# Kept key products, a scaled state on ScalarE, and reordered attention projections in a two-layer hybrid backbone

## The chip, the cores and the metric

The program runs on one core of one Trainium2 chip. Its metric is the device time of one execution in microseconds (us). A core has TensorE (PE, with its weight loads shown as PEld), VectorE (DVE), ScalarE (ACT), GpSimd (POOL) and the DMA queues, most of them issued by SyncE (SP). The engines run side by side, each through its own list of instructions in order, and meet only at semaphores.

## The reference

One inference step of a two-layer backbone, for 512 latent tokens and 128 context tokens together (640 columns). Each layer runs three head groups on one normalised input: a bidirectional chunked gated DeltaNet, latent attention (MLA), and windowed attention with a sink. Their outputs go through one projection, and a squared-ReLU MLP follows. The change is in the preparation of the two attentions and in the DeltaNet recurrence:

```python
kb = kc * bc[..., None]
lower = jnp.where(strict, jnp.einsum('nbhik,nbhjk->nbhij', kb, kc) * decay, 0.0)
...
intra = jnp.where(incl, jnp.einsum('nbhik,nbhjk->nbhij', qc, kc) * decay, 0.0)
def step(S, inp):
    v_new = u_i - jnp.einsum('bhck,bhkv->bhcv', w_i, S)
    o_i = (jnp.einsum('bhck,bhkv->bhcv', q_i * jnp.exp(g_i)[..., None], S)
           + jnp.einsum('bhij,bhjv->bhiv', a_i, v_new))
    S = (S * jnp.exp(g_last)[..., None]
         + jnp.einsum('bhck,bhcv->bhkv', k_i * jnp.exp(g_last - g_i)[..., None], v_new))
...
q_m = (_rms_norm(m_cq, g) @ w_uq)         # per head 64 plain columns and 32 that are rotated
q_rope = _apply_rope(q_rope, cos_m, sin_m)
k_nope, v_m = _mla_expand(ckv_n, w_ukv)
```

The recurrence runs forward over the latent blocks and, with its own decays, backward. The products `k k^T` and `q k^T` of a block are the same for both directions.

## The kernel before, in words

All activations are feature-major: 128 features on the partitions, tokens in the columns. The kernel works in blocks of 128 tokens: four latent blocks 0 to 3 and the context block 4 (`LB` is 4, `NB` is 5). Every engine has its list written out by hand, and `wait_ge` and `then_inc` on named semaphores tie the lists together; a wait holds back all that stands behind it on its engine. No scheduler moves anything.

**Attention preparation** (lines 2588 to 2655 on TensorE, 1233 to 1265 on ScalarE, 1976 to 1991 on VectorE). TensorE turns the values and keys of the DeltaNet into token-major form (`QKV`, `KTOK`), multiplies latent keys and queries by a permutation (`rr`) so that VectorE can rotate them with `rotate(n, ...)` (`rot`), and then projects: `queries` three times (two groups of plain columns, then the rotated columns `QR`), `keys` twice, the values `VM` and the turned window values `SVT`. ScalarE copies each result out of PSUM (`pev`). The rotated queries `QR` go from ScalarE to a permutation on TensorE, to VectorE (`rotate(4, ...)`), and to GpSimd, which copies them into `QT` (`qrc`). Then the score matmuls `scores_a` (L2660) begin.

**Attention rounds** follow: eight rounds of scores, softmax, turned weights and values, then the context block.

**Recurrence.** `blocks[s]` gives the block of step s for direction d: forward 0, 1, 2, 3 and backward 3, 2, 1, 0, and both take block 4 at the end. In one step (loop `for s in range(LB - 1)`) the state part of step s and the preparation of step i = s + 1 are interleaved:

- TensorE: `key_state` (L2860, state times grown keys `KE`), `key_products(i, 0)` (L2748), `solve` (L2873), `key_products(i, 1)`, `query_state` (L2882), `first_product(i, 0)` (L2763), `update` (L2898), `corner_product`, `second_product`, `own_values` (L2890).
- VectorE: `right_side` (`XS`), `scaled_decays` (`DTB`, L2092), `decayed(i, 0)` (`CM` and `AT` from the key products in PSUM, L2107), `solution` (`VN`, L2168), `decayed(i, 1)`, `masked` (`DT`, L2084), `state` (`SS`, L2188: four instructions, each old state times its decay plus the update), `output` (`OACC`), and small copies between.
- GpSimd: `KE` and `QE` (L858), `VS` (L890), and the spreads `UU` and `TT` (L842, L850).
- ScalarE: the decays (`gate_less`, `gate_grown`, `gate_decay`) and half of the small copies.

`first_product(i, 0)` waits for `CM` and `AT` of both directions (`cm`, `atm`). The next `key_state` waits for the state (`sst`) and for the output copied out of the bank that it writes (`oa`).

Step i = 1 needs the products of blocks 1 and 2, step 2 those of 2 and 1, step 3 those of 3 and 0: in steps 2 and 3 TensorE makes again what steps 0 and 1 had. The weight buffer `RAW` holds two chunks of 1 MB and `X` the residual input; `refill(g)` loads chunk g + 2 into `RAW[g % 2]`.

## Time and profile before

| | |
|---|---|
| median of 3 runs | 1798.57 us (1796.0 to 1802.94) |
| the profiled execution | 1795.4 us, of it the span of the profile 1793.6 us |
| busy share of the span | PE 96%, PEld 92%, DVE 70%, ACT 47%, POOL 29% |
| mean granted TensorE clock | 0.99 |

The page gives the span in engines, in 40 slices, in a chain of waits and in groups of instructions. Layer 0 prepares its attentions at 261 to 283 us, runs the rounds to 350 and the recurrence to 425; layer 1 does the same at 1139 to 1161, 1228 and 1303. A timeline row gives start and length of a group of like instructions, and in brackets the idle time of the engine ahead of it with what ended it. The end of a row of matmuls lies a little over the start of the next row, since matmuls are pipelined.

### The profile page before, as it was taken

How to read it: one execution, taken by the hardware profiler on the slowest of the kernel's cores; microseconds unless marked ns; L12 is line 12 of the kernel's file. 1: busy time of each engine (PE TensorE's matmuls, PEld its weight loads, DVE VectorE, ACT ScalarE, POOL GpSimd, SP SyncE). 2: the span in 40 equal slices, each digit the busy share in tenths (PEclk: the TensorE clock that was granted, in tenths of full speed). 3: DMA queues.
4: the chain of work that ended last, by engine and by line, in shares of the span. 5: the costliest groups of instructions: out<-in, count | busy, mean ns of one | idle time of the engine just before them, and what ended most of it. 6: DMA issues, size and time to landing. Idle time of an engine off the chain costs nothing.

```text
span 1793.6 us, 33484 instructions
## 1 busy us (share of the span) xinstructions
PE 1730.5 (96%) x13554; PEld 1649.8 (92%) x13554; DVE 1263.6 (70%) x2087; ACT 846.4 (47%) x1455; POOL 521.8 (29%) x418
## 2 busy tenths in 40 slices
PE   5999999999999999999999999999999999999997
PEld 2889996789999999999999999778899999999997
DVE  2688776798635776776665557668987777788885
ACT  1555427744342231322325653476446665756663
POOL 5000002174441140421551000215822323333235
PEclk9999999999999999999999999999999999999998
DMA  8653213023557779687527861651133677887662
GB/s 341 255 211 104 79 60 83 2 67 120 202 190 244 290 222 336 234 269 290 182 71 213 187 147 48 141 95 55 38 112 118 218 252 234 306 291 244 225 205 83
DMA packets 128037, 316.66 MB, mean 177 GB/s; under 512 B 37828, under 2 KB 64236, under 8 KB 108172
## 3 DMA queue, kind: packets, MB, share of 16 engines
q1 hardware_dynamic: 121740, 279.49, 44.6%
q0 software_dynamic: 4608, 33.56, 9.6%
q8 instruction: 108, 1.77, 0.4%
q10 hardware_dynamic: 1536, 1.48, 0.2%
q14 instruction: 45, 0.37, 0.1%
HBM read 286.01 MB, written 95.49 MB: 213 GB/s over the span
## 4 chain that ended last, share of the span: by engine, by line
PE 82%; DVE 8%; DMA 3%; issue 3%; ACT 3%; SPq 1%; POOL 0%; POOLq 0%; DVEq 0%; ACTq 0%
PE PS L2389 48%; PE PS L2458 19%; DMA ADA<-ada 1%; PE PS L2660 1%; PE PS L2748 1%; PE PS L2706 1%; PE PS L2685 1%; PE PS L2890 1%; PE PS L2674 1%; DVE MPR L1812 1%; PE PS L2526 1%; PE PS L2694 1%; PE PS L2898 1%; PE PS L2873 1%; PE PS L2860 1%
## 5 line engine op out<-in xcount | busy, mean ns | idle before, releaser
L2389 PE MATMUL PS<-HH,HI 128*128 128x320 f32 (+1 forms) x1280 | 299.9, 316 | 5.2 <-DVE HL L1561 5.2
L2389 PE MATMUL PS<-HL,HI 128*128 128x320 f32 (+1 forms) x1280 | 295.4, 312 | 0.0
L2389 PE MATMUL PS<-HH,LO 128*128 128x320 f32 (+1 forms) x1280 | 293.5, 310 | 0.0
L957 ACT CAST HI<-RAW 128x2048 fp32r<-128x2048 f32 x64 | 121.9, 1904 | 274.0 <-PE PS L2389 246.8
L2389 PEld LDWEIGHTS PS<-HH,HI 128*128 128x128 f32 x1280 | 215.3, 190 | 5.8 <-issue 5.7
L2389 PEld LDWEIGHTS PS<-HL,HI 128*128 128x128 f32 x1280 | 219.3, 191 | 0.0
L2389 PEld LDWEIGHTS PS<-HH,LO 128*128 128x128 f32 x1280 | 217.1, 190 | 0.0
L2458 PE MATMUL PS<-FB,WHL 128*128 128x320 f32 x1344 | 199.4, 309 | 5.3 <-DVE TMP L1689 2.4
L2458 PE MATMUL PS<-HB,WHL 128*128 128x322 f32 (+1 forms) x1344 | 202.5, 313 | 2.1 <-DVE TMP L1689 1.5
L2458 PEld LDWEIGHTS PS<-FB,WHL 128*128 128x128 f32 x1344 | 197.1, 188 | 7.6 <-DVE WHL L1606 5.4
L2458 PEld LDWEIGHTS PS<-HB,WHL 128*128 128x128 f32 x1344 | 201.7, 191 | 2.4 <-issue 2.4
L1004 ACT CAST WHL<-RAWB 128x512 fp32r<-128x512 f32 x224 | 137.7, 618 | 111.3 <-PE PS L2458 92.7
L1552 DVE TENSOR_TENSOR LO<-RAW,HI 128x2048 fp32r<-128x2048 f32 x62 | 149.0, 2404 | 56.1 <-ACT HI L957 55.8
L2389 PE MATMUL PS<-FH,HI 128*128 128x320 f32 x768 | 175.8, 310 | 1.6 <-issue 1.6
L1606 DVE TENSOR_TENSOR WHL<-RAWB,WHL 128x512 fp32r<-128x512 f32 x224 | 168.6, 778 | 8.9 <-ACT WHL L1004 7.3
L2389 PE MATMUL PS<-FH,LO 128*128 128x320 f32 x768 | 174.6, 309 | 0.0
L2389 PE MATMUL PS<-FL,HI 128*128 128x320 f32 x640 | 145.7, 309 | 0.0
L1812 DVE SCALAR_TENSOR_TENSOR MPR<-WM,CB 128x1024 f32<-128x1024 f32 x96 | 137.9, 1437 | 9.5 <-DMA WM<-adt 7.8
L2389 PEld LDWEIGHTS PS<-FH,HI 128*128 128x128 f32 x768 | 127.9, 188 | 2.0 <-issue 1.1
L2389 PEld LDWEIGHTS PS<-FH,LO 128*128 128x128 f32 x768 | 128.3, 188 | 0.0
L2389 PEld LDWEIGHTS PS<-FL,HI 128*128 128x128 f32 x640 | 107.1, 188 | 0.0
L933 POOL TENSOR_TENSOR TC<-TC 128x640 f32<-128x640 f32 x32 | 50.4, 1576 | 181.3 <-ACT FH L1497 181.3
(380 smaller groups left out, 2874.9 us busy)
## 6 DMA issues: line engine op xcount, KB each, us to landing
RAW<-ws SPq DMA_DIRECT2D x64, 1024.0 KB, 5.1
wp<-ws SPq DMA_DIRECT2D x32, 1024.0 KB, 8.2
RAWB<-wp SPq DMA_DIRECT2D x128, 256.0 KB, 4.0
WM<-adt SPq DMA_DIRECT2D x48, 512.0 KB, 9.2
RAWB<-ws SPq DMA_DIRECT2D x96, 256.0 KB, 3.9
FS<-hb SPq DMA_DIRECT2D x28, 640.0 KB, 8.6
ADA<-ada SPq DMA_DIRECT2D x16, 1024.0 KB, 7.8
wp<-ws POOLq DMA_DIRECT2D x16, 1024.0 KB, 10.1
```

The source lines that it names most:

```text
L933: nc.gpsimd.tensor_tensor(TC[u][:, 0:T], TC[u][:, 0:T], TC[u][:, 0:T], ALU.mult).then_inc(S["f1_sq"], 1)
L957: nc.scalar.copy(HI[g % 2][:, :], RAW[g % 2][:, :]).then_inc(hi_ready, 1)
L1004: nc.scalar.copy(WHL[:, w % SLOTS, 0, :], operand(w)).then_inc(F["whi"], 1)
L1552: last = nc.vector.tensor_tensor(LO[g % 2][:, c], RAW[g % 2][:, c], HI[g % 2][:, c].bitcast(F32), ALU.subtract)
L1606: nc.vector.tensor_tensor(WHL[:, w % SLOTS, 1, :], operand(w), WHL[:, w % SLOTS, 0, :].bitcast(F32), ALU.subtract).then_inc(F["wlo"], 1)
L1812: return nc.vector.scalar_tensor_tensor(out=MPR[:, :], in0=w[:, :], scalar=1.0, in1=cond[:, g, :], op0=ALU.mult, op1=ALU.mult, accum_out=M ...
L2389: last = pe.matmul(bank(2 * u + a)[:, 0:e], w[:, cols], m[:, a * HT:a * HT + e], start=(k == 0 and f), stop=(k == KT - 1 and e_))
L2458: last = pe.matmul(out, x[:, cols], B[:, y, k, 0:n], start=(opens and k == 0 and v == 0), stop=(k == H - 1 and v == 2), skip_group_check=n ...
L2526: last = pe.matmul(bank(7)[:, 464 + i * NB + b:465 + i * NB + b], SQT[i % 2][:, c.start - 1:c.stop - 1], one, start=True, stop=True)
L2660: pe.matmul(pair(0)[:, 0:LAT], q, kt[:, 0:LAT], start=True, stop=True)
L2674: last = pe.matmul(bank(7 if i else 2)[:, c:c + hi - lo], TSQ[rows, p, toks(b)], KSW[rows, lo:hi], start=True, stop=True)
L2685: last = pe.transpose(pair(2)[:, toks(i)], TC[a % 2][:, toks(slot)], ident)
```

## The change

Five edits, in both layers:

1. ScalarE copies the key products of steps 0 and 1 out of PSUM into four SBUF tiles `KK` (`products_out`, by block), and TensorE makes none for steps 2 and 3. `decayed(2, ...)` and `decayed(3, ...)` read `KK`. `decayed` of step 1 and of (0, 0) waits for ScalarE's copies; TensorE waits for them too at four places (`kte` + 5, 6, 8).
2. ScalarE multiplies the state by its decay beforehand (`state_decay`, four instructions into `SD`), and `state` on VectorE is one addition.
3. The rotated queries are projected first; their copy, permutation and rotation come before the other queries and keys; waits stand later or are split, and one new one is there (`rot` + 5 before the second `keys`).
4. The last copy of turned values on ScalarE goes ahead of the last projection tile's bias activations.
5. `KK` and `SD` lie in `RAW[0]` and in `X`, so the load of chunk 12 and the load of half of `X` are issued later.

```diff
+        KK = [place(f"KK{b}", [P, H, 2, P], F32, w) for b, w in enumerate((r_raw, r_x, r_x + 4096, r_raw + 4096))]
+        SD = [place(f"SD{d}", [P, H, P], F32, (r_x + 8192, r_kd)[d]) for d in range(2)]
 ... SyncE
-                        if s % 2 == 0 and s // 2 + 1 < PT_ // 2 - 1:
+                        if s % 2 == 0 and s // 2 + 1 < PT_ // 2 - 2:
                             refill(g0 + s // 2 + 1)
...
-                    sp.dma_start(X[:, 0:4, :, :], ...)
                     for i in range(2, NB):
                         ...
                         gates_in(i)
+                    sp.wait_ge(S["cm"], o["cm"] + 8)
+                    sp.wait_ge(S["atm"], o["atm"] + 8)
+                    refill(g0 + 10)
+                    sp.wait_ge(S["sst"], o["sst"] + 11)
+                    sp.dma_start(X[:, 0:4, :, :], ...)
 ... ScalarE
+                        if j == PT_:
+                            values_out(j - 21)
                         if j >= 1:
                             tile_out(j - 1)
...
+                    def products_out(i, d):
+                        act.wait_ge(S["kk"], o["kk"] + 2 * i + d + 1)
+                        if i == 0 and d == 1:
+                            act.wait_ge(S["atm"], o["atm"] + 2)
+                        c, e = kk_bank(i, d)
+                        for a in range(2):
+                            last = nc.scalar.copy(KK[blocks[i][d]][:, 2 * a:2 * a + 2, :, :],
+                                                  bank(c + e * a).rearrange("p (h q c) -> p h q c", h=2, q=2))
+                        last.then_inc(S["kte"], 1)
+                    def state_decay(s, d):
+                        ...
+                        for h in range(H):
+                            last = nc.scalar.activation(SD[d][:, h, :], SS[d][:, h, :], ACT.Identity,
+                                                        scale=SMALL[:, 5, n + h:n + h + 1])
+                        last.then_inc(S["sst"], 1)
 ... VectorE
-                    dve.wait_ge(S["pev"], o["pev"] + 3)
+                    dve.wait_ge(S["pev"], o["pev"] + 1)
                     rotate(4, every, QR[:, 0:LAT], 0, QR[:, 0:LAT])
...
-                        dve.wait_ge(S["kk"], o["kk"] + min(v + 1, 9))
+                        if i == LB or v == 1:
+                            dve.wait_ge(S["kk"], o["kk"] + min(v + 1, 5))
+                        else:
+                            dve.wait_ge(S["kte"], o["kte"] + min(v + 5, 8))
...
-                            if e == 1:
+                            if 1 < i < LB:
+                                last = nc.vector.tensor_tensor(out[d][:, :, :], KK[blocks[i][d]][:, :, q, :], x[d][:, :, :], ALU.mult)
+                            elif e == 1:
...
-                        for h in range(H):
-                            x = SS[d][:, h, :]
-                            last = nc.vector.scalar_tensor_tensor(out=x, in0=x, scalar=egt[...],
-                                                                  in1=hb(4 * d + 1)[:, h, :], op0=ALU.mult, op1=ALU.add)
+                        dve.wait_ge(S["sst"], o["sst"] + 4 * s + 2)
+                        nc.vector.tensor_tensor(SS[d][:, :, :], SD[d][:, :, :], hb(4 * d + 1), ALU.add).then_inc(S["sst"], 1)
 ... TensorE
-                        key_products(i, 0)
+                        if i == 1:
+                            key_products(i, 0)
                         solve(s, 0)
                         solve(s, 1)
-                        key_products(i, 1)
+                        if i == 1:
+                            key_products(i, 1)
                         query_state(s, 0)
                         query_state(s, 1)
+                        if i == 1:
+                            pe.wait_ge(S["kte"], o["kte"] + 8)
                         first_product(i, 0)
```

TensorE's attention preparation, layer 0, before, from the third query projection (`WUQ`, the rotated columns) over the keys (`WUKV`, `CKC`) to the permutation of `QR`; two other query projections stand ahead.

```order
L2614 MATMUL PS<-TCQ_65,WUQ_177 128x512 x2
L2614 MATMUL PS<-TCQ_65,WUQ_177 128x128 x2
L2618 MATMUL PS<-TCKV_66,WUKV_178 128x512
L2619 MATMUL PS<-TCKV_66,WUKV_178 128x128
L2620 MATMUL PS<-CKC_179,WUKV_178 128x128
L2618 MATMUL PS<-TCKV_66,WUKV_178 128x512
L2619 MATMUL PS<-TCKV_66,WUKV_178 128x128
L2620 MATMUL PS<-CKC_179,WUKV_178 128x128
L2633 MATMUL PS<-QR_190,K_49 128x512
```

The changed kernel, from its second query projection on; the first, ahead of it, is that of the rotated columns:

```order
L2665 MATMUL PS<-TCQ_65,WUQ_183 128x512 x2
L2665 MATMUL PS<-TCQ_65,WUQ_183 128x128 x2
L2677 MATMUL PS<-QR_196,K_49 128x512
L2669 MATMUL PS<-TCKV_66,WUKV_184 128x512
L2670 MATMUL PS<-TCKV_66,WUKV_184 128x128
L2671 MATMUL PS<-CKC_185,WUKV_184 128x128
L2665 MATMUL PS<-TCQ_65,WUQ_183 128x512 x2
L2665 MATMUL PS<-TCQ_65,WUQ_183 128x128 x2
L2669 MATMUL PS<-TCKV_66,WUKV_184 128x512
L2670 MATMUL PS<-TCKV_66,WUKV_184 128x128
L2671 MATMUL PS<-CKC_185,WUKV_184 128x128
```

The permutation of `QR` moved from the end to directly behind the first two query projections.

TensorE, the step that begins at 376.90 us in layer 0, before: `SS,KE` is `key_state`, `QKV` the key products, `XS,UU` `solve`, `SS,QE` `query_state`, `TT,CM` the start of `first_product`.

```order
L2860 MATMUL PS<-SS0_173,KE0_147 128x128 x4
L2860 MATMUL PS<-SS1_174,KE1_148 128x128 x4
L2748 MATMUL PS<-QKV_62 128x256 x4
L2873 MATMUL PS<-XS0_130,UU00_165 128x128 x4
L2873 MATMUL PS<-XS1_131,UU01_166 128x128 x4
L2748 MATMUL PS<-QKV_62 128x256 x4
L2882 MATMUL PS<-SS0_173,QE0_149 128x128 x4
L2882 MATMUL PS<-SS1_174,QE1_150 128x128 x4
L2763 MATMUL PS<-TT0_169,CM0_157 32x32 x2
```

The same place of the changed kernel:

```order
L2908 MATMUL PS<-SS0_173,KE0_147 128x128 x4
L2908 MATMUL PS<-SS1_174,KE1_148 128x128 x4
L2921 MATMUL PS<-XS0_130,UU00_165 128x128 x4
L2921 MATMUL PS<-XS1_131,UU01_166 128x128 x4
L2930 MATMUL PS<-SS0_173,QE0_149 128x128 x4
L2930 MATMUL PS<-SS1_174,QE1_150 128x128 x4
L2811 MATMUL PS<-TT0_169,CM0_157 32x32 x2
```

Both rows of key products are gone, and nothing stands in their place between `query_state` and `first_product`.

ScalarE between the context's weights and the second inversion of step 0, before:

```order
L1371 COPY TMP0_98<-PS 128x512
L1374 COPY PTB0_199<-PS 128x512
L1273 ACTIVATE DT0_137<-EG10_134,SMALL_102 128x128 x4
L1273 ACTIVATE DT1_138<-EG11_135,SMALL_102 128x128 x4
L1379 COPY RNBC_203<-PS 128x512
L1339 COPY TT01_156<-PS 32x4x32 x2
L1347 COPY UU01_166<-PS 32x4x32 x2
L1281 ACTIVATE EG10_134<-EG10_134 128x512
L1281 ACTIVATE EG11_135<-EG11_135 128x512
L1347 COPY UU01_166<-PS 64x4x64
```

The changed kernel:

```order
L1358 COPY KK0_175<-PS 128x512 x2
L1411 COPY TMP0_98<-PS 128x512
L1414 COPY PTB0_205<-PS 128x512
L1358 COPY KK3_178<-PS 128x512 x2
L1290 ACTIVATE DT0_137<-EG10_134,SMALL_102 128x128 x4
L1419 COPY RNBC_209<-PS 128x512
L1379 COPY TT01_156<-PS 32x4x32 x2
L1387 COPY UU01_166<-PS 32x4x32 x2
L1290 ACTIVATE DT1_138<-EG11_135,SMALL_102 128x128 x4
L1298 ACTIVATE EG10_134<-EG10_134 128x512
L1298 ACTIVATE EG11_135<-EG11_135 128x512
L1387 COPY UU01_166<-PS 64x4x64
```

Two double copies of key products stand ahead of the first decay of step 1, and the second decay went behind the small copies `TT` and `UU`.

## Rows read from the trace of the kernel before

**Rows 1.** Mean over stretches, two recurrence steps, layer 0: busy PE, PEld, DVE, ACT, POOL; clock, DMA, GB/s.
```profile
377.00:408.30 31.30, 31.30 (x448) 28.88 (x449) 29.37 (x59) 11.73 (x33) 25.84 (x21) 1.00 0.07 21
```

**Rows 2.** Timeline of TensorE, one recurrence step, layer 0: start, length (us), what, count.
```profile
376.90 2.05 PE L2860 MATMUL PS<-SS,KE 128*128 128x128 f32 x16
...
378.79 1.89 PE L2748 MATMUL PS<-QKV 128*128 128x256 f32 x8
...
385.91 0.46 PE L2763 MATMUL PS<-TT,CM 128*32 128x32 f32 x32
...
392.58 2.12 PE L2860 MATMUL PS<-SS,KE 128*128 128x128 f32 x16
```

**Rows 3.** Timeline of VectorE, the same step.
```profile
379.60 2.36 DVE L2092 TENSOR_TENSOR DTB<-DT,SMALL 128x512 f32<-128x512 f32 x2
...
383.08 1.27 DVE L2168 TENSOR_TENSOR VN<-PS,SMALL 128x512 f32<-128x512 f32 x2
...
384.28 0.68 DVE L2107 TENSOR_TENSOR CM<-PS,DTB 128x512 f32<-128x512 f32 x1
...
385.47 0.95 DVE L2084 TENSOR_TENSOR DT<-DT,K 128x512 f32<-128x512 f32 x1
...
389.37 1.12 DVE L2188 SCALAR_TENSOR_TENSOR SS<-SS,SMALL,PS 128x128 f32<-128x128 f32 x4
...
391.77 0.68 DVE L2178 COPY OACC<-PS 128x512 f32<-128x512 f32 x1
```

**Rows 4.** Timeline of GpSimd, the same step; in brackets the idle time ahead.
```profile
378.46 2.95 POOL L858 TENSOR_TENSOR KE<-QKV,EG 128x512 f32<-128x512 f32 x2
...
383.83 2.04 POOL L890 TENSOR_TENSOR VS<-VN,SMALL 128x512 f32<-128x512 f32 x2 [2.43 <-DVE VN L2168]
...
385.83 3.39 POOL L858 TENSOR_TENSOR QE<-QKV,EG 128x512 f32<-128x512 f32 x2
```

**Rows 5.** Timeline of VectorE, where GpSimd stands still.
```profile
364.80 1.47 DVE L2092 TENSOR_TENSOR DTB<-DT,SMALL 128x512 f32<-128x512 f32 x2
```

**Rows 6.** Timeline of GpSimd around it.
```profile
368.14 2.04 POOL L890 TENSOR_TENSOR VS<-VN,SMALL 128x512 f32<-128x512 f32 x2 [3.81 <-DVE VN L2168]
```

**Rows 7.** Timeline of TensorE, start of the recurrence.
```profile
356.59 1.16 PE L2860 MATMUL PS<-SS,KE 128*128 128x128 f32 x8
...
365.56 1.89 PE L2748 MATMUL PS<-QKV 128*128 128x256 f32 x8
```

**Rows 8.** Timeline of VectorE, start of the recurrence.
```profile
355.08 0.75 DVE L2112 TENSOR_TENSOR AT<-PS,DT 128x256 f32<-128x256 f32 x2
...
368.57 0.68 DVE L2107 TENSOR_TENSOR CM<-PS,DTB 128x512 f32<-128x512 f32 x1
```

**Rows 9.** Timeline of ScalarE, one copy of 128x512 out of PSUM.
```profile
352.74 0.59 ACT L1371 COPY TMP<-PS 128x512 f32<-128x512 f32 x1 [1.53 <-PE PS L2815]
```

**Rows 10.** Timeline of TensorE, attention preparation of layer 0.
```profile
263.35 0.77 PE L2594 MATMUL PS<-K,QKV 128*128 128x128 f32 x5 [1.61 <-ACT QKV L1239]
...
282.99 1.10 PE L2660 MATMUL PS<-KTT,QT 96*128 96x512 f32 x2 [0.93 <-ACT SVT L1265]
```

**Rows 11.** Timeline of VectorE, the last rotation.
```profile
279.05 0.69 DVE L1980 TENSOR_TENSOR RP<-QR,ROT 128x512 f32<-128x512 f32 x1 [3.64 <-PE PS L2633]
```

**Rows 12.** Stretches of layer 1, TensorE: busy, granted clock, DMA share, GB/s.
```profile
1372.00:1374.00 2.00, 1.43 (x9) 0.61 0.53 149
...
1374.00:1376.00 2.00, 2.00 (x9) 0.50 0.66 211
...
1378.00:1380.00 2.00, 2.00 (x12) 0.68 0.79 179
```

**Rows 13.** Timeline of TensorE there.
```profile
1371.35 1.28 PE L2411 MATMUL PS<-K,SQ 128*128 128x1 f32 x10
...
1373.20 5.17 PE L2458 MATMUL PS<-HB,WHL 128*128 128x322 f32 x18 [0.57 <-ACT E L1052]
```

**Rows 14.** DMA issues of the page: KB each, us to landing.
```profile
RAW<-ws SPq DMA_DIRECT2D x64, 1024.0 KB, 5.1
```

More of the change, by code:

```diff
@@ L1165, in tile_out, with values_out @@
                                                  scale=VEC[:, V_W + 12 + q:V_W + 13 + q]).then_inc(S["tap"], 1)
+                    def values_out(h):
+                        act.wait_ge(S["vtr"], o["vtr"] + h + 1)
+                        nc.scalar.copy(QKV[:, 8 + h, 0:T], pair(2)).then_inc(S["vte"], 1)
                     def conv_silu(i):
@@ L1247, in _, with queries_out, keys_out @@
                         nc.scalar.copy(KTOK[:, h, :], pair(3 - h % 2)).then_inc(S["kte"], 1)
-                    for n in range(2):
-                        act.wait_ge(S["pmm"], o["pmm"] + n + 1)
-                        nc.scalar.activation(QT[0:NOPE, 2 * n, :], pair(3 - n)[0:NOPE, :], ACT.Identity, scale=MSCALE)
-                        nc.scalar.activation(QT[0:NOPE, 2 * n + 1, :], pair(3 - n)[NOPE:2 * NOPE, :], ACT.Identity,
+                    def queries_out(n):
+                        act.wait_ge(S["pmm"], o["pmm"] + 2 * n + 2)
+                        nc.scalar.activation(QT[0:NOPE, 2 * n, :], pair(2)[0:NOPE, :], ACT.Identity, scale=MSCALE)
+                        nc.scalar.activation(QT[0:NOPE, 2 * n + 1, :], pair(2)[NOPE:2 * NOPE, :], ACT.Identity,
                                              scale=MSCALE).then_inc(S["pev"], 1)
-                    act.wait_ge(S["pmm"], o["pmm"] + 3)
+                    def keys_out(n):
+                        act.wait_ge(S["pmm"], o["pmm"] + 2 * n + 3)
+                        src = pair(3 * n, T + PAST)
+                        nc.scalar.copy(KTT[0:NOPE, 2 * n, :], src[0:NOPE, :])
+                        nc.scalar.copy(KTT[0:NOPE, 2 * n + 1, :], src[NOPE:2 * NOPE, :]).then_inc(S["pev"], 1)
+                    act.wait_ge(S["pmm"], o["pmm"] + 1)
                     nc.scalar.activation(QR[:, :], pair(3), ACT.Identity, scale=MSCALE).then_inc(S["pev"], 1)
                     for n in range(2):
-                        act.wait_ge(S["pmm"], o["pmm"] + n + 4)
-                        src = pair(2 * (1 - n), T + PAST)
-                        nc.scalar.copy(KTT[0:NOPE, 2 * n, :], src[0:NOPE, :])
-                        nc.scalar.copy(KTT[0:NOPE, 2 * n + 1, :], src[NOPE:2 * NOPE, :]).then_inc(S["pev"], 1)
+                        queries_out(n)
+                        keys_out(n)
                     for n in range(3):
@@ L2621, in _ @@
                     pe.wait_ge(S["kte"], o["kte"] + 3)
-                    queries(pair(3), slice(0, P)).then_inc(S["pmm"], 1)
+                    queries(pair(3), slice(2 * P, 3 * P)).then_inc(S["pmm"], 1)
                     pe.wait_ge(S["kte"], o["kte"] + 4)
-                    queries(pair(2), slice(P, 2 * P)).then_inc(S["pmm"], 1)
+                    queries(pair(2), slice(0, P)).then_inc(S["pmm"], 1)
                     pe.wait_ge(S["pev"], o["pev"] + 1)
-                    queries(pair(3), slice(2 * P, 3 * P)).then_inc(S["pmm"], 1)
-                    pe.wait_ge(S["pev"], o["pev"] + 2)
-                    keys(pair(2, T + PAST), slice(0, P)).then_inc(S["pmm"], 1)
+                    pe.matmul(bank(7), pm[0], QR[:, 0:LAT], start=True, stop=True).then_inc(S["rr"], 1)
                     pe.wait_ge(S["rot"], o["rot"] + 1)
                     pe.wait_ge(S["rot"], o["rot"] + 2)
-                    keys(pair(0, T + PAST), slice(P, 2 * P)).then_inc(S["pmm"], 1)
-                    pe.wait_ge(S["pev"], o["pev"] + 3)
-                    pe.matmul(bank(7), pm[0], QR[:, 0:LAT], start=True, stop=True).then_inc(S["rr"], 1)
-                    pe.wait_ge(S["rot"], o["rot"] + 4)
+                    keys(pair(0, T + PAST), slice(0, P)).then_inc(S["pmm"], 1)
+                    pe.wait_ge(S["pev"], o["pev"] + 2)
+                    queries(pair(2), slice(P, 2 * P)).then_inc(S["pmm"], 1)
+                    pe.wait_ge(S["rot"], o["rot"] + 5)
+                    keys(pair(3, T + PAST), slice(P, 2 * P)).then_inc(S["pmm"], 1)
                     for n in range(3):
+                        if n == 2:
+                            pe.wait_ge(S["pev"], o["pev"] + 5)
                         for b in range(2 * n, 2 * n + 2):
@@ L2913, in _ @@
                         scores_a(2 * r)
+                        if r == 0:
+                            pe.wait_ge(S["pev"], o["pev"] + 9)
                         if r:
```

45 lines of the change are left out of this document (27 added, 18 removed).

## The prediction

> **What bounds the kernel now.** I read the busy shares first: TensorE 96% of the span, so a TensorE instruction that goes should be time that goes. Then I asked the stage itself. In the two middle recurrence steps of layer 0, TensorE is busy for all of 31.30 us, but VectorE for 29.37 and GpSimd for 25.84 [rows 1]. Two or three engines run almost in step there, and the reader is to see that the busy share of one of them doesn't name the bound. The timelines of one step do: TensorE begins a step with `key_state` at 376.90 and the next at 392.58, 15.68 us later [rows 2]. VectorE's `OACC` copy, which `key_state` waits for, begins at 391.77 and is 0.68 long [rows 3]: it is out at 392.4, and `key_state` starts at 392.58. So TensorE and VectorE come to the end of the step within 0.2 us of each other. If TensorE loses work, VectorE stays.
>
> Third I compared VectorE's operations with themselves. `DTB`, both inputs in SBUF, takes 1.47 for two at 364.80 [rows 5], where GpSimd stands idle until 368.14 [rows 6]. The same two take 2.36 at 379.60 [rows 3] while GpSimd makes `KE` from 378.46 to 381.41 [rows 4]; they end at 381.96, 0.55 after GpSimd. `DT` at 385.47, also two SBUF inputs, takes 0.95 and ends at 386.42, 0.55 after `VS` of GpSimd ends at 385.87 [rows 3, 4]. `CM` at 384.28 with an input in PSUM takes 0.68 in the middle of that same `VS`. I read this as: an operation with two SBUF inputs waits until GpSimd's running instruction is over, one with a PSUM input doesn't.
>
> **Key products (edit 1).** TensorE loses 4 groups of 1.89 per layer [rows 2], less the 0.16 that each lies over the next: 1.73, so 6.9 per layer and 13.8 in all, if TensorE were the only bound. Against it stand 4 pairs of `CM` and `AT` per layer that now read two SBUF tiles. Worked out on step 1 of layer 0: `CM` and `AT` of direction 0 fall where GpSimd waits for `VN` (idle 2.43 until 383.83 [rows 4]) and keep their 0.60 between starts. `VN` runs 383.08 to 384.28. Then direction 1: `VS` has two instructions of 1.02. `CM` is wanted at 384.28, waits for the first until 384.85 and ends at 385.4; the second `VS` runs to 386.4, and `AT` ends at 386.95, where it ended at 385.47. The next GpSimd instruction (`QE`, some 1.2) gets in, and `DT` ends at 388.7 instead of 386.42. The second `DT` follows another `QE`. By then VectorE is some 2.2 behind.
>
> **State (edit 2).** Four instructions of together 1.12 become one of 0.68 as in the `OACC` row, per direction [rows 3]: 0.44 twice, 0.9 per step back. `SD` is made on ScalarE, four instructions a direction, between the steps; ScalarE is busy 11.73 of 31.30 [rows 1], so it is hidden. Step net: 2.2 - 0.9 = 1.3. Bounds: -0.9, if reading `KK` costs nothing, and +1.7, if GpSimd also falls behind; I take 1.2, because every two-input row read above shows the wait. Two such steps per layer: **+2.4**.
>
> **Start of the recurrence.** VectorE's last `AT` of step 0 ends at 355.83 [rows 8]. Only then may ScalarE copy bank 0, two copies of 0.59 [rows 9], and `key_state(0, 0)`, now at 356.59 [rows 7], waits for them: 355.8 + 1.1 + 0.1 = 357.0, 0.4 late. ScalarE has 2.4 more of copies and 1.2 of `SD` queued ahead of the decays, and `CM` of direction 1, at 368.57 now [rows 8], waits for a copy of products that end at 365.56 + 1.89 = 367.45 [rows 7]. With the copy behind them that is 368.6, and the 0.4 and the later decays come on top. Step 0 also has its 0.9 back from `SS`, but TensorE has 6.67 of work from `first_product` to `key_state` (385.91 to 392.58 [rows 2]) that doesn't shrink. Between +0.4 and +1.5 I take **+0.9** per layer.
>
> **Preparation (edits 3 and 4).** TensorE idles 1.61 before 263.35 for ScalarE's copy [rows 10]; that copy now goes ahead of two activations and 1.3 of the 1.61 go. The 0.93 before the scores at 282.99 [rows 10] go as well, since that wait stands after the first scores now. In their place comes `rot` + 5: VectorE's other rotations end 3.64 before 279.05, at 275.4 [rows 11], and the fifth takes three operations, to 277.4. TensorE reaches the second keys at about 276.2, so 1.2 of waiting is new. Net 1.3 + 0.9 - 1.2 = **-1.0** per layer (between 0 and -1.3). It passes on whole, since each round of attention hangs on the one before.
>
> **Loads (edit 5).** Chunk 12 is loaded when VectorE has done `decayed(3, 1)`, and takes 5.1 [rows 14]; its user on ScalarE comes some 6 later. Hidden, by about 1. `X` is used after the recurrence. Cost nothing; price if the cover fails, up to 2 per layer.
>
> Sum without the clock: 2.4 + 0.9 - 1.0 = 2.3 per layer, **+4.6**.
>
> **The clock.** TensorE's query products of step 1 end 3.46 earlier, at about 382.4, and `first_product`, now at 385.91, must wait for the late `AT`: 387.0. Between them TensorE has nothing in its list: an idle gap of 4.5 us, in two steps of each layer. No idle time of the profile's warm part comes near it. What does come near: in layer 1 TensorE worked on single-column products ([rows 13], the second row of ten at 1371.35), idled 0.57 to 1373.20, and the granted clock fell. It is 0.61 in 1372 to 1374, 0.50 to 1376 and 0.68 in 1378 to 1380 [rows 12]: from 1372.4 to 1379.3 at the lower level of 1.2 GHz, 6.8 us. TensorE then works through the 6.67 us from `first_product` to `key_state` at half speed for 4.6 to 6.8 us (a fall early in the gap has part of it behind it), losing 2.3 to 3.4, less 0.3 that VectorE would have been late anyway. I take 2.1 in each of four gaps (bounds 0 and 3.1): **+8.4**. The Trainium skill, TensorE: Matmul & The Clock Gate (HAM oscillation), warns that idle gaps between bursts of matmuls put the array back to the low clock. The row above shows it for a stretch of little work, none for a gap.
>
> From the Trainium skill, GPSIMD Engine Reference (Key points), comes a rule that speaks against edit 1: GpSimd shares its SBUF interfaces with VectorE and contends with its instructions that have two SBUF inputs. Its page VectorE: DVE Perf Modes (The TRN2 errata) gives VectorE a smaller fixed cost from SBUF than from PSUM; by that alone reading `KK` would be no dearer and a step would cost -0.9; by the first it costs what is above. The rows side with the first.
>
> The profiled execution is 1795.4 (span 1793.6 and 1.8 around it), 3.2 below the median of 1798.57. The terms are differences, so I put them on the median: 1798.6 + 4.6 + 8.4 = **1811.6**; I say 1811. No change is within 0.5%, 9.0 us.
>
> **Rivals.** (a) The two-input wait is there, the clock holds: +4.6, 1803.2. For it: nothing in the trace shows a gap of pure idleness with a fall behind it. Against: the stretch that did make it fall was busier than the gap. Chance 0.17. (b) Faster or equal: `KK` reads as fast as PSUM, because GpSimd mostly finds its gaps elsewhere; then steps give 0.9 back each. 0.9 - 1.8 - 1.0 = -1.9 per layer, -3.8: 1794.8. It decides from whether `CM` and `AT` stay under 0.7; the row of `DTB` speaks against it. TensorE's gap shrinks to some 3.4, and the clock may fall nevertheless. Chance 0.12. (c) TensorE alone is the bound, VectorE's lateness isn't: 13.8 and 2.0 go, 1782.8. The 0.2 us between `OACC` and `key_state` speaks against it. Chance 0.03. (d) Worse: chunk 12 lands late or GpSimd becomes a bound that carries into the last step, another 2 per layer: 1816. For it: GpSimd has 25.84 of 31.30 and is held by VectorE in turn (`QE` 3.39 against `KE` 2.95 [rows 4]). Chance 0.08.
>
> **Numbers.** Forecast 0.60, its own range 1806 to 1817 (clock falls in two to four gaps at 2 to 3). Slower by over 0.5%: 0.51 of the forecast, 0.07 of (d), 0.01 of (a): 0.59. Same: 0.09 of the forecast, 0.16 of (a), 0.09 of (b), 0.01 of (d): 0.35. Faster: 0.03 of (b), 0.03 of (c): 0.06. Range 1799 to 1819.
>
> **What would show it.** `CM` and `AT` from `KK` longer than 0.7 and ending 0.5 after a GpSimd instruction; at 0.6 the step term is wrong. `SS` at 0.68 each. TensorE idle 4 to 5 us before two `first_product` in each layer; the steps 17 long, not 15.7. Granted clock of 0.5 for some 6.8 us behind these gaps; at 1.0 there rival (a) holds. `key_state(0, 0)` half a microsecond after the copies. First scores of the attention 1.0 earlier against the last projection. A step under 15 us would make the forecast wrong as a whole.

## The result, and the profile after the change

Over 18 runs each, the changed kernel takes a median of 1804.34 us (1800.95 to 1807.12) and the kernel before 1797.36 us (1794.95 to 1802.94). The medians are 7.0 apart. The ratio on record is 1.0035, with a 95% interval of 1.0028 to 1.0041, or 6.3 us more (5.0 to 7.4). It is slower, as forecast, but by half of the forecast 12.4, and by less than the 9.0 us that were called a change. The time lies in the stated range, but nearer to rival (a)'s 1803.2 than to the 1811; 1.2 us of its distance to 1811 come from the kernel before, whose median is 1797.36 over 18 runs where the forecast built on 1798.57. The profiled execution has a span of 1801.7 us where before's was 1793.6, 8.1 more.

TensorE's timeline of the same step of layer 0 answers to [rows 2]. The `key_state` row opens the step.

```profile
377.62 2.12 PE L2908 MATMUL PS<-SS,KE 128*128 128x128 f32 x16
...
381.52 1.95 PE L2930 MATMUL PS<-SS,QE 128*128 128x128 f32 x16
388.03 0.66 PE L2811 MATMUL PS<-TT,CM 128*32 128x32 f32 x32 [4.57 <-DVE AT L2158]
...
396.35 2.12 PE L2908 MATMUL PS<-SS,KE 128*128 128x128 f32 x16
...
400.25 1.95 PE L2930 MATMUL PS<-SS,QE 128*128 128x128 f32 x16
406.20 0.65 PE L2811 MATMUL PS<-TT,CM 128*32 128x32 f32 x32 [4.01 <-DVE AT L2158]
...
414.08 1.89 PE L2796 MATMUL PS<-QKV 128*128 128x256 f32 x8
```

The step is 18.73 us long (377.62 to 396.35), before 15.68; the next is 17.73 to the key products of step 4 at 414.08. The reader is to see the two gaps: 4.57 and 4.01 us of idle ahead of `first_product` (the row with the 128x32 tiles), both ended by VectorE's `AT`. VectorE's timeline of the step answers to [rows 3], GpSimd's to [rows 4].

```profile
382.89 0.68 DVE L2158 TENSOR_TENSOR CM<-KK,DTB 128x512 f32<-128x512 f32 x1
383.49 0.68 DVE L2158 TENSOR_TENSOR AT<-KK,DT 128x512 f32<-128x512 f32 x1
...
385.30 1.15 DVE L2158 TENSOR_TENSOR CM<-KK,DTB 128x512 f32<-128x512 f32 x1
386.36 1.52 DVE L2158 TENSOR_TENSOR AT<-KK,DT 128x512 f32<-128x512 f32 x1
387.81 1.76 DVE L2133 TENSOR_TENSOR DT<-DT,K 128x512 f32<-128x512 f32 x1
...
389.69 1.55 DVE L2133 TENSOR_TENSOR DT<-DT,K 128x512 f32<-128x512 f32 x1
...
392.59 0.69 DVE L2241 TENSOR_TENSOR SS<-SD,PS 128x512 f32<-128x512 f32 x1
```

```profile
379.47 2.95 POOL L864 TENSOR_TENSOR KE<-QKV,EG 128x512 f32<-128x512 f32 x2
384.85 2.49 POOL L896 TENSOR_TENSOR VS<-VN,SMALL 128x512 f32<-128x512 f32 x2 [2.43 <-DVE VN L2222]
```

`CM` and `AT` of direction 0 read `KK` while GpSimd waits for `VN`, from 382.42 to 384.85: 0.68 each, as from PSUM. Those of direction 1 meet its two `VS`, and take 1.15 and 1.52; the masked `DT` behind them take 1.76 and 1.55, where they took 0.95 ([rows 3]) and 1.14. `VS` itself goes from 2.04 to 2.49. `AT` is out at 387.88, 10.26 after `key_state`; TensorE, with its products gone, has been idle since 383.46.

The clock, in stretches of TensorE around the first gap and the second: length and busy time, granted clock, DMA share, GB/s.

```profile
385.00:386.00 1.00, 0.00 (x0) 0.74 0.00 0
386.00:392.00 6.00, 3.97 (x105) 0.50 0.02 5
392.00:393.00 1.00, 1.00 (x8) 0.84 0.60 179
405.00:406.00 1.00, 0.00 (x0) 0.98 0.00 0
406.00:409.00 3.00, 2.79 (x56) 0.50 0.52 177
409.00:410.00 1.00, 1.00 (x66) 0.81 1.02 434
```

A mean of 0.74 over one microsecond is 0.52 us at the lower level, so the first fall runs from 385.5 to 392.3 (6.83 us). It begins 2.0 us after TensorE had run dry, and 4.3 of it are left when `first_product` starts. The second runs from 406.0 to 409.4 (3.41 us), 3.8 after TensorE had run dry, and 3.2 are left. The same gaps and falls stand in layer 1 (1266.1 to 1272.9 and 1286.6 to 1290.0), with 4.6 and 3.3 left. The lower clock doesn't double everything: the group of 128x32 products takes 0.66 for 0.46, the update behind it 2.08 for 1.16.

The preparation, against [rows 10]: the last projection ahead of it and the first scores behind it (first and last row below) are 22.80 us apart before (260.19 and 282.99) and 22.12 after. The start of the recurrence, against [rows 7], in the last row.

```profile
261.29 0.46 PE L2440 MATMUL PS<-HH,LO 128*128 128x320 f32 x2
...
263.07 0.77 PE L2645 MATMUL PS<-K,QKV 128*128 128x128 f32 x5 [0.24 <-ACT QKV L1176]
...
266.31 0.77 PE L2645 MATMUL PS<-K,QKV 128*128 128x128 f32 x5 [0.44 <-ACT KTOK L1258]
...
278.64 1.13 PE L2669 MATMUL PS<-TCKV,WUKV 128*128 128x512 f32 x2 [0.64 <-DVE QR L2031]
...
283.41 1.02 PE L2708 MATMUL PS<-KTT,QT 96*128 96x512 f32 x2
```

```profile
357.40 1.16 PE L2908 MATMUL PS<-SS,KE 128*128 128x128 f32 x8 [0.38 <-ACT KK L1358]
```

The stretch is 0.68 shorter, and 0.66 in layer 1 (22.79 to 22.13), where 1.0 was forecast. The idle time fell by more, 1.22: waits of 1.61 and 0.93 are gone, and 0.24, 0.44 (for `KTOK`) and 0.64 (for the fifth rotation) have come. The rest went into the products themselves: the ten of `WUKV,TCKV` take 2.55 for 2.32, and each idle time undoes an overlap of about 0.16 with the row before it. In layer 1 there is no wait for `KTOK`, and the one for the rotation is longer:

```profile
1158.94 1.13 PE L2669 MATMUL PS<-TCKV,WUKV 128*128 128x512 f32 x2 [1.32 <-DVE QR L2031]
```

The second keys, which wait for the rotation, start 17.35 behind the last projection in layer 0 and 17.36 in layer 1: the wait for `KTOK` costs nothing.

At the start of the recurrence, `key_state(0, 0)` is 0.84 behind `first_product` instead of 0.39; to the next `first_product` it is 14.49 instead of 13.80, so 0.69.

I count the recurrence in intervals from one `first_product` to the next and to its end (the first product of the output stage):

| kernel, layer | 0 to 1 | 1 to 2 | 2 to 3 | 3 to 4 | 4 to end | sum |
|---|---|---|---|---|---|---|
| before, 0 | 13.80 | 15.91 | 15.75 | 10.81 | 12.73 | 69.00 |
| before, 1 | 13.81 | 16.46 | 15.65 | 10.65 | 12.72 | 69.29 |
| after, 0 | 14.49 | 16.98 | 18.17 | 11.48 | 12.56 | 73.68 |
| after, 1 | 14.49 | 16.99 | 18.34 | 11.53 | 12.55 | 73.90 |

### The profile page after: what moved, and what is told of

It is laid out like the page before. It is cut to its first block, busy times and chain, and to the rows that moved or that the text cites. A ratio compares the mean times of both kernels' runs of the same rounds, so it can differ in the third digit from the quotient of the medians.

```text
span 1801.7 us, 33400 instructions
## 1 busy us (share of the span) xinstructions
PE 1721.7 (96%) x13490; PEld 1639.9 (91%) x13490; DVE 1268.0 (70%) x2051; ACT 868.9 (48%) x1519; POOL 523.7 (29%) x418
## 4 chain that ended last, share of the span: by engine, by line
PE 83%; DVE 7%; DMA 3%; ACT 3%; issue 3%; SPq 1%; POOL 0%; POOLq 0%; ACTq 0%; DVEq 0%
PE PS L2440 50%; PE PS L2509 18%; DMA ADA<-ada 2%; PE PS L2708 1%; PE PS L2946 1%; PE PS L2938 1%; DVE WHL L1655 1%; PE PS L2754 1%; PE PS L2577 1%; PE PS L2733 1%; PE PS L2722 1%; PE PS L2742 1%; PE PS L2796 1%; PE PS L2766 1%; DMA leaf<-LM 1%
## 5 line engine op out<-in xcount | busy, mean ns | idle before, releaser
L1861 DVE SCALAR_TENSOR_TENSOR MPR<-WM,CB 128x1024 f32<-128x1024 f32 x96 | 137.9, 1437 | 15.4 <-DMA WM<-adt 13.8
```

The lines of the kernel that those rows point to most:

```text
L1861: return nc.vector.scalar_tensor_tensor(out=MPR[:, :], in0=w[:, :], scalar=1.0, in1=cond[:, g, :], op0=ALU.mult, op1=ALU.mult, accum_out=M ...
```

## The experiments

All times are medians; the ratio is the one on record, to runs of the kernel before on the same chip, and it can differ by up to 0.0006 from that of the two medians. **One: is it the clock or VectorE?** The gap is filled with the old products, which no longer count up `kk` in these steps.

```diff
-                        if i == 1:
-                            key_products(i, 0)
+                        key_products(i, 0)
...
-                        if i == 1:
-                            key_products(i, 1)
+                        key_products(i, 1)
```

> The changed kernel, but TensorE still computes the key products of steps 2 and 3 as well, at their old places in its order; nobody reads them. VectorE still reads KK. Theory (the clock falls in the gap and costs about 1.65 and 1.24 us in the two middle steps of a layer): the gap ahead of first_product shrinks from 4.6 to about 1.1 us, the granted clock stays 1.0, first_product starts where it did (10.4 us after key_state), and key_state follows 6.7 us later; 5.8 us of the changed kernel's 7 over before go, ratio to before 1.0005 to 1.001. Rival (the time goes to VectorE's lateness alone, the clock is beside the point): steps stay 18.7 and 17.7, ratio 1.0035 to 1.004.

Measured: 1803.43 us over 5 runs, ratio 1.0033 (1.0020 to 1.0045): by the time alone, the rival's number. The trace says otherwise. TensorE's rows of this kernel:

```profile
388.62 0.46 PE L2812 MATMUL PS<-TT,CM 128*32 128x32 f32 x32 [1.25 <-DVE AT L2158]
...
405.70 0.46 PE L2812 MATMUL PS<-TT,CM 128*32 128x32 f32 x32 [0.70 <-DVE AT L2158]
...
412.64 0.34 PE L2837 MATMUL PS<-UU,PQ 128*64 128x64 f32 x4 [0.77 <-issue]
...
420.70 0.29 PE L2837 MATMUL PS<-UU,PQ 128*32 128x32 f32 x6 [1.34 <-issue]
```

The gap is 1.25, the clock stayed at 1.0 through both middle steps, and they shrank as the theory said (17.08 where the changed kernel has 18.17). But TensorE stood still late in the recurrence for 0.77 and 1.34 us that the profile puts down to `issue`: it shows nothing that the engine waited for. Behind the second the clock fell (0.50 from 421 to 424). Layer 1 had 0.85 and 0.28 of such idle. The answer needed a kernel with fewer instructions.

**Two: the same gap, half the instructions.**

```diff
+                    def filler(i, d):
+                        pe.wait_ge(S["um"], o["um"] + i * NL * 2)
+                        for n in range(2):
+                            pe.matmul(bank(4 * d + 2), QKV[:, 4 + n, cblk(0)], QKV[:, n, 0:512], start=True, stop=True)
...
                         if i == 1:
                             key_products(i, 0)
+                        else:
+                            filler(i, 0)
```

(and the same for direction 1.)

> As fill, but in place of the eight unread key products of steps 2 and 3 TensorE makes four products of 512 columns, the same time with half the instructions. In fill the trace showed full clock behind the gaps, but idle of 0.77, 1.34 and 0.85 us put down to issue in the last step of the recurrence while X and chunk 12 were loading, and a clock fall behind the 1.34. Theory (the clock falls cost 1.7 to 2.0 us per layer, and fill lost that again to late code): no such idle here, from the first first_product to the end of the recurrence 71.8 to 72.2 us per layer (73.7 and 73.9 in the changed kernel, 69.0 in before), ratio to before 1.0015. Rival (filling costs that much in any case): 73 and more, ratio 1.003 to 1.0035.

Measured: 1799.97 us, ratio 1.0009 (0.9999 to 1.0020). TensorE's rows, then the clock in stretches over both filled gaps:

```profile
389.33 0.46 PE L2817 MATMUL PS<-TT,CM 128*32 128x32 f32 x32 [1.29 <-DVE AT L2158]
...
396.55 2.12 PE L2914 MATMUL PS<-SS,KE 128*128 128x128 f32 x16
...
406.41 0.46 PE L2817 MATMUL PS<-TT,CM 128*32 128x32 f32 x32 [0.73 <-DVE AT L2158]
...
421.26 0.68 PE L2817 MATMUL PS<-TT,CM 128*64 128x64 f32 x15 [0.84 <-issue]
```

```profile
384.00:396.00 12.00, 10.20 (x181) 1.00 0.17 47
400.00:412.00 12.00, 10.76 (x173) 1.00 0.26 89
```

The clock holds. Intervals of layer 1: 14.49, 16.98, 17.08, 10.82, 12.56, sum 71.93. Layer 0 agrees up to its last interval (14.49, 16.99, 17.08, 10.83, 13.50). Against the changed kernel's 73.68 in layer 0 and 73.90 in layer 1, the clock falls cost 1.75 and 1.97 us, 3.7 in all; the two ratios to before differ by 0.0026, or 4.7, with an interval of 1 to 2 us to each side of either. Layer 0's longer last interval holds 0.84 of `issue`, so this part of the expectation failed.

**Three: is it the reads?** Nothing is changed but where `CM` and `AT` read; the values of steps 2 and 3 are of other products.

```diff
-                            if 1 < i < LB:
+                            if False:
```

> The changed kernel, but CM and AT of steps 2 and 3 read the PSUM banks that key products had before the change (old contents, so these products are of wrong numbers); the copies to KK stay, TensorE's key products of these steps stay left out. Theory (the wait of a two-SBUF operation for GpSimd's running instruction is what makes VectorE late): CM and AT take 0.68 each, AT ends some 2.2 to 2.5 us earlier against key_state, TensorE's gap is about 3 us; if the clock holds there, ratio 0.997 to 0.998, if it falls 0.9995 to 1.001. Rival (VectorE is late for another cause, such as the waits for ScalarE's SD and KK): CM and AT at 0.68 but first_product still 10.4 us after key_state, ratio 1.003 or more.

Measured: 1799.73 us, ratio 1.0011 (1.0002 to 1.0020). VectorE's timeline of the step, direction 1 (`key_state` at 378.47), and TensorE's two gaps:

```profile
386.14 0.68 DVE L2161 TENSOR_TENSOR CM<-PS,DTB 128x512 f32<-128x512 f32 x1
386.74 0.68 DVE L2161 TENSOR_TENSOR AT<-PS,DT 128x512 f32<-128x512 f32 x1
387.33 0.95 DVE L2133 TENSOR_TENSOR DT<-DT,K 128x512 f32<-128x512 f32 x1
```

```profile
387.56 0.66 PE L2811 MATMUL PS<-TT,CM 128*32 128x32 f32 x32 [3.24 <-DVE AT L2161]
...
403.97 0.46 PE L2811 MATMUL PS<-TT,CM 128*32 128x32 f32 x32 [2.69 <-DVE AT L2161]
```

The same sizes in the same order from another memory: 0.68 for all four, and `first_product` 9.09 behind `key_state`, not 10.41. The interval 1 to 2 is 15.66 where the filled kernel has 16.99: the reads cost 1.33 us in that step. The ratio is the one expected for the case that the clock falls; that of the rival, 1.003, is out. The clock fell at both gaps of layer 0 (from 387.4 and 404.5) and in the first of layer 1, 3.23 long, but not at the second there, 2.69 long.

**Four: the state alone, and without.** `decay` is before with edit 2, `nodecay` the changed kernel without it:

```diff
-                        dve.wait_ge(S["sst"], o["sst"] + 4 * s + 2)
-                        nc.vector.tensor_tensor(SS[d][:, :, :], SD[d][:, :, :], hb(4 * d + 1), ALU.add).then_inc(S["sst"], 1)
+                        for h in range(H):
+                            x = SS[d][:, h, :]
+                            last = nc.vector.scalar_tensor_tensor(out=x, in0=x, scalar=egt[:, blocks[s][d], d, h:h + 1],
+                                                                  in1=hb(4 * d + 1)[:, h, :], op0=ALU.mult, op1=ALU.add)
+                        last.then_inc(S["sst"], 1)
```

> Before with edit 2 alone (the state is decayed on ScalarE, VectorE adds), with the later load of X that it needs. Theory: VectorE is 0.9 us shorter per step, but TensorE stands 0.2 us behind it in the middle steps, so these give at most 0.2 each; the last step gives 0.7 as in the changed kernel, since VectorE's CM and AT are what its first_product waits for: 1.5 to 2.5 us in all, ratio 0.9985 to 0.999. Rival (the last step's 0.7 came from elsewhere, such as key products and KK): ratio 0.9995 to 1.000.

> The changed kernel without edit 2: the state is decayed and summed by VectorE in four instructions, as before. Theory (in the changed kernel VectorE sets the pace of the steps, so what edit 2 takes off it counts): 0.9 us per step longer in the steps behind two state sums, 1.8 to 2.7 per layer; ratio to before 1.0055 to 1.0065. Rival (as in before, where edit 2 alone gave 0.9997, TensorE or GpSimd cover it): ratio 1.0035.

Measured: `decay` 1797.41 us, ratio 0.9997 (0.9988 to 1.0005), `nodecay` 1803.89 us, 1.0031 (1.0021 to 1.0042). Neither is to be told from its partner. The theory for `nodecay`, 1.0055 and more, is out. That for `decay`, 0.9985 to 0.999, is not quite out by the time, but its trace has the rival: sums of 68.82 and 68.84 against 69.00 and 69.29 (0.54 of them `issue`), and no 0.7 in the last step (10.88 and 10.76 from 3 to 4, before 10.81 and 10.65). In `nodecay` the state sums take 0.43 more each, and this is all that comes of it:

```profile
375.07 1.12 DVE L2224 SCALAR_TENSOR_TENSOR SS<-SS,SMALL,PS 128x128 f32<-128x128 f32 x4
```

```profile
371.40 0.46 PE L2796 MATMUL PS<-TT,CM 128*32 128x32 f32 x32 [0.80 <-DVE AT L2143]
...
378.26 2.05 PE L2893 MATMUL PS<-SS,KE 128*128 128x128 f32 x16
...
388.39 0.65 PE L2796 MATMUL PS<-TT,CM 128*32 128x32 f32 x32 [4.35 <-DVE AT L2140]
```

The interval 1 to 2 is 16.99 against 16.98 with edit 2: `key_state` starts 6.86 behind `first_product` instead of 6.57, and the next `first_product` comes 0.28 sooner behind it. In layer 1 all five intervals agree within 0.01. In layer 0 the interval 2 to 3 is 18.41 for 18.17, but there the clock fell 0.5 us later against `first_product`, and 4.8 us of the fall were left, not 4.3.

**Five: the preparation alone** (edits 3 and 4 on before: the values' copy moved up, rope queries first).

> Before with the reordered preparation alone (edits 3 and 4). Theory: 0.8 to 1.0 us per layer come back and stay, 1.6 to 2.0 in all, ratio 0.999. Rival (the first waits of attention take them back): 1.000.

Measured: 1794.59 us, ratio 0.9980 (0.9970 to 0.9991). The recurrence is 68.83 in both layers. The traces show 0.7 per layer for the preparation and 0.2 and 0.5 in the recurrence, where before has 0.54 of `issue` in layer 1: 2.1 in all. The medians differ by 3.4, and the ratio's interval is 1.6 to 5.4 us; the rival's 1.000 is out.

**Six: out of the way of `VS`.** In `order` VectorE makes `CM` and `AT` of direction 1 ahead of `VN`; in `order_swap` the updates also trade places with the own values; in `order_swap_half` half the filler is added to that.

```diff
                         decayed(i, 0)
+                        if i > 1:
+                            decayed(i, 1)
                         solution(s, 0)
                         solution(s, 1)
-                        decayed(i, 1)
+                        if i == 1:
+                            decayed(i, 1)
```

> The changed kernel, but in steps 2 and 3 VectorE makes CM and AT of direction 1 right behind those of direction 0, ahead of the two VN, while GpSimd still waits for VN and stands still. Theory (only GpSimd's running VS makes them long): all four at 0.68 or less, first_product 2.4 us earlier (14.6 behind the one before, not 17.0), TensorE's gap about 2 us; VS and update come 1.2 later, so half of it is given back: from the first first_product to the end 69.5 to 70.5 us if the clock holds, 71 to 71.5 if it falls; ratio 0.9985 to 1.0005. Rival (the wait only moves on, to the masked DT that follow): the four short but no step shorter, ratio 1.003.

> As order, and in steps 2 and 3 TensorE makes the own values (which need VN) in the places of the updates (which need VS) and the updates in theirs, with VectorE's copies and state sums exchanged to match. Theory (what order gives back is the wait of update for VS): 1.0 us less per step than order, 67.5 to 69 us from the first first_product to the end, ratio 0.996 to 0.998. Rival (GpSimd's own row of KE, VS, QE and the two spreads is the bound by then): no shorter than order, ratio as there.

> As order_swap, with two unread products of 512 columns (1.7 us) ahead of the query products of steps 2 and 3, so that the gap of 2.1 us is filled. In order_swap the clock fell in both gaps and once more in the last step. Theory (with the clock held the reordered steps are as short as those of before): first_product 14.5 and 15.7 us behind the one before, the last step 11 to 12, 69 to 70.5 us in all, ratio 0.998 to 1.000. Rival (the last step's 13.2 and 13.8 are VectorE's and GpSimd's own, not the clock's): 71.5 or more, ratio 1.001.

The second and third of them add, on TensorE, the exchange (and the same on VectorE), and the third alone the last line, behind `if i == 1: ... else:`:

```diff
-                        update(s, 0)
+                        early, late = (own_values, update) if i > 1 else (update, own_values)
+                        early(s, 0)
...
+                            filler(i, 1)
```

Measured: 1801.91 us, ratio 1.0024 (1.0014 to 1.0033); 1800.96, 1.0017 (1.0008 to 1.0025); 1802.51, 1.0026 (1.0017 to 1.0035). TensorE in `order`, layer 1, then the two rows of `order_swap_half` that matter:

```profile
1266.01 0.46 PE L2814 MATMUL PS<-TT,CM 128*32 128x32 f32 x32 [2.09 <-DVE AT L2158]
1267.64 2.07 PE L2949 MATMUL PS<-VS,KTOK 128*128 128x128 f32 x8 [1.17 <-POOL VS L896]
...
1296.27 0.46 PE L2814 MATMUL PS<-TT,CM 128*32 128x32 f32 x32 [0.58 <-DVE CM L2161]
```

```profile
1283.93 0.46 PE L2821 MATMUL PS<-TT,CM 128*32 128x32 f32 x32 [1.61 <-DVE AT L2158]
...
1297.13 0.46 PE L2821 MATMUL PS<-TT,CM 128*32 128x32 f32 x32 [1.97 <-DVE CM L2161]
```

All three theories of the time failed: 1.0005, 0.998 and 1.000 were their upper ends. The reads are short and the interval 1 to 2 is 14.5, as expected. What it gave came back: `update` waits 1.17 for `VS`, the clock fell in three of the four gaps of `order`, and the interval 3 to 4 went from 11.5 to 13.2 and 13.4. In `order_swap_half` the clock held through layer 1 until 1298, and the interval 3 to 4 is 13.20 all the same: there the rival was right, it isn't the clock that sets it. TensorE waits 1.61 and 1.97 for VectorE's `AT` and `CM`, so the lateness only moved. The sums of layers 0 and 1 are 73.35 and 71.98 in `order`, 73.66 and 72.70 in `order_swap`, 72.92 and 72.69 in `order_swap_half`.

**Seven: keep one direction.** `KK` for direction 0, whose reads fall where GpSimd waits; direction 1 stays with TensorE and PSUM.

```diff
-                    products_out(0, 0)
...
-                            if 1 < i < LB:
+                            if 1 < i < LB and d == 0:
...
-                        if i == 1:
-                            key_products(i, 1)
+                        key_products(i, 1)
```

> The changed kernel, but key products are kept for direction 0 alone: in steps 2 and 3 CM and AT of direction 0 read KK (there GpSimd waits for VN), those of direction 1 read PSUM, and TensorE still computes their products. Theory (GpSimd's VS lengthens only the reads of direction 1, and a gap of 1.5 us or less keeps the clock): CM and AT all at 0.68, first_product 15.65 us behind the one before as with the old PSUM contents, from the first first_product to the end 69.1 to 69.6 us; with the preparation's gain ratio 0.998 to 0.999. If the clock falls here too: 70.5 to 71, ratio 0.9995 to 1.0005. Rival (keeping products costs by its copies or loads, not by the reads of direction 1): 71.5 or more, ratio 1.002.

Measured: 1794.47 us, ratio 0.9980 (0.9971 to 0.9989).

```profile
385.26 0.68 DVE L2159 TENSOR_TENSOR CM<-PS,DTB 128x512 f32<-128x512 f32 x1
385.86 0.68 DVE L2159 TENSOR_TENSOR AT<-PS,DT 128x512 f32<-128x512 f32 x1
```

```profile
386.68 0.46 PE L2809 MATMUL PS<-TT,CM 128*32 128x32 f32 x32 [1.30 <-DVE AT L2159]
...
402.35 0.46 PE L2809 MATMUL PS<-TT,CM 128*32 128x32 f32 x32 [1.52 <-DVE AT L2159]
...
417.24 0.68 PE L2809 MATMUL PS<-TT,CM 128*64 128x64 f32 x15 [0.57 <-issue]
```

All at 0.68 (those of direction 0 too, at 382.86 and 383.46), gaps of 1.30 and 1.52, the clock at 1.0. The sums are 69.40 in layer 1 and 69.96 in layer 0, of which 0.57 is `issue`. By the time it is as fast as the preparation alone and no faster; its recurrence in layer 1 is 0.57 longer than that kernel's 68.83, since the start costs 0.68 and the steps give only 0.1 back. 1.7 us less of TensorE per step buy nothing, because VectorE needs 8.7 to 9.0 us from `key_state` to `AT` either way (377.81 to 386.54 and 393.25 to 402.22), and before, with all its products, TensorE took 9.01 for the same stretch (376.90 to 385.91).

**Eight: two checks.** `prep_decay` is before with edits 2 to 4. `fill_xlate` is `fill_wide` with:

```diff
-                    sp.wait_ge(S["sst"], o["sst"] + 11)
-                    sp.dma_start(X[:, 0:4, :, :], t["xs"][:, 0:4] if l else t["xT"][:, 0:4]).then_inc(S["xa"], 16)
...
                     refill(g0 + 11)
+                    sp.wait_ge(S["om"], o["om"] + 2 * LB)
+                    sp.dma_start(X[:, 0:4, :, :], t["xs"][:, 0:4] if l else t["xT"][:, 0:4]).then_inc(S["xa"], 16)
```

> Before with edits 2, 3 and 4: the preparation reordered and the state decayed on ScalarE, no key products kept. Theory (edit 2 gives 0 to 0.5 us per layer, the preparation 1 per layer and what its own run showed beyond): ratio 0.9975 to 0.9985, not to be told from the preparation alone (0.998). Rival (the two add up, edit 2 gives 0.9 per step once the preparation is out of the way): ratio 0.996.

> As fill_wide, but X is loaded only after the last own values, behind the load that frees at step 4, so not while the recurrence runs. In fill_wide one of two layers had 0.84 us of idle put down to issue, 5 us after the load of X began. Theory (code for TensorE comes late where X and two weight chunks load back to back): no idle put down to issue in either layer, 71.9 us in both, 0.5 to 1 us off fill_wide's time, ratio 1.0005. Rival (that idle is chance or the program's length): it is seen again in one of the layers, ratio 1.001.

Measured: 1793.90 us, ratio 0.9979 (0.9970 to 0.9987), and 1799.64 us, 1.0013 (1.0004 to 1.0022). The first is the lowest median of all and cannot be told from the preparation alone; the rival's 0.996 is out. In the second the idle put down to `issue` is there again (0.82 up to 420.09 in layer 0), so the load of `X` doesn't cause it. Such idle was seen in the recurrences of `fill`, `fill_wide`, `fill_xlate`, `nodecay` and `one`, and in layer 1 of before, which keeps no key products; it was not seen in the changed kernel itself. The traces have a hint that no experiment followed up. Each of these nine idle times ends 1.24 to 1.50 us after a load of 16 KB of instructions has landed (queue q8 of the DMA: at 419.83 in `fill_wide`, where TensorE goes on at 421.26; at 415.78 and 417.24 in `one`; at 1250.36 and 1251.69 in before). This fits instructions that come late. But most such loads, some nine in every recurrence, are followed by no idle time, so why these came late stays open.

## Why the prediction was half right

Per layer, forecast and measured, in us:

| term | forecast | measured | from |
|---|---|---|---|
| preparation | -1.0 | -0.68, -0.66 | last projection to first scores |
| start, step 0 | +0.9 | +0.69, +0.68 | interval 0 to 1 |
| two middle steps, full clock | +2.4 | +2.41, +1.95 | intervals 1 to 3, `fill_wide` less before |
| clock | +4.2 | +1.75, +1.97 | sum of after less `fill_wide` layer 1 |
| last step | 0 | -0.16, 0.0 | intervals from 3 on, `fill_wide` layer 1 less before |
| sum | +6.5 | +4.0, +3.9 | |

(In layer 1 before has 0.54 of `issue` idle in the interval 1 to 2, hence 1.95 and not 2.49.) Both layers together are 8.0, and the profiled spans differ by 8.1. The ratio gives 6.3 (5.0 to 7.4) and the medians 7.0; the distance to 8.0 isn't explained. One profiled execution also differs from another by falls of the clock elsewhere: between 50 and 1770 us before has three of 6.8 us (from 218.7, 1096.0 and 1372.4), and the changed kernel, outside its recurrences, four of 3.4 (from 74.9, 126.1, 221.6 and 1102.3). No run prices these.

**What bounds the kernel, and the key products (edit 1): right.** VectorE stayed, and TensorE's 13.8 us bought nothing. The operations of direction 1 wait for GpSimd and end 0.55 after it: `VS` ran in two of 1.02 and longer from 384.85, `CM` and `AT` took 1.15 and 1.52 where I had 1.12 and 1.55, and `stale` shows that the memory read is all that matters. The rule of the Trainium skill on the shared SBUF interfaces (GPSIMD Engine Reference, Key points) agrees; the smaller fixed cost of SBUF reads (VectorE: DVE Perf Modes, The TRN2 errata) shows nothing here, 0.68 from either.

**State (edit 2): wrong, and hidden in a right sum.** I took 0.9 per step back from VectorE's shorter sums. `nodecay` shows 0.0, and `decay` 0.0 to 0.24. These sums lie beside TensorE's own work between `first_product` and `key_state`. A step is two halves with different limits: from `key_state` to `first_product` VectorE sets the time, from there to `key_state` TensorE and the exchanges with it do. The wait was over-charged by as much: `stale` prices the reads at 1.33 in one step, where I had 2.2 for VectorE and passed all of it on. The 1.2 that I took was right by luck. Rival (b) has the same fault: without the wait a step gives nothing, not 0.9 (15.66 against 15.91 and 15.75).

**The clock: right in kind, twice too dear.** This is the step that made the forecast wrong: 8.4 was its term, and 3.7 was measured, while the other terms, forecast at 4.6, came to 4.2. All four gaps are there, 4.57 and 4.01 for 4.5, and the clock fell in each. So rival (a), a clock that holds, is out as a mechanism, though its 1803.2 is the nearest number to the 1804.34. The rows that I leaned on were misread in one point: the clock of [rows 12] began to fall at 1372.45, 0.2 ahead of the idle time of 0.57 [rows 13]. I took 2.1 per gap, and the falls cost 1.09 and 0.65 in layer 0 and 1.26 and 0.71 in layer 1. Four sizes were off. The first fall began 2.0 us into the gap, so 2.5 of its 6.8 us were spent in idleness. The second lasted 3.4, not 6.8: the one length that [rows 12] show was taken for all. The lower clock doesn't take half of TensorE's speed in this stretch: 4.3 us of it would then have cost 2.1, and they cost 1.65. So TensorE's work from `first_product` on grew by 1.65 (8.32 for 6.67) and 1.24 (7.88 for 6.64), where I had 2.3 to 3.4. And 0.55 of each lay beside VectorE, not 0.3: at full clock, in `fill_wide`, the same stretch takes 7.22, since TensorE waits twice, 0.25 and 0.26, for VectorE's copies behind the late masked `DT`; with the lower clock these waits are gone. 8.32 less 7.22 is 1.10, 7.88 less 7.22 is 0.66. Layer 1 bears this out: there 4.6 and 3.3 us of the falls were left for TensorE's work, not 4.3 and 3.2, and both cost more. What the Trainium skill says of gaps between bursts (TensorE: Matmul & The Clock Gate, HAM oscillation) is borne out by the granted clock here; its cost is not to be had from TensorE alone.

**Start, preparation, loads.** The start was as forecast, 0.69 for 0.9: `key_state(0, 0)` came 0.45 later against `first_product`, 0.4 was said. The preparation gave 0.7 instead of 1.0. The fifth rotation holds up the second keys as I said, 17.35 behind the last projection where I had 17.2. The rest is behind it: 0.2 for the ten products that take 2.55 instead of 2.32, and 0.1 for the first product of the keys, 1.13 instead of 1.02. Why these got longer isn't shown. Rival (d) is out: no wait in the changed kernel is for chunk 12. Rival (c) is out as well: TensorE lost its products and the time rose.
